# Feed-forward units two by two over two PSUM banks, and the rotation done on raw tiles ahead of the head norm

## The reference, cut to what matters

```python
def rmsnorm(x, w):
    y = xf * lax.rsqrt(jnp.mean(xf * xf, axis=-1, keepdims=True) + EPS) * w
def rope(x, pos):
    x1, x2 = xf[..., : hd // 2], xf[..., hd // 2:]
    return concatenate([x1 * cos - x2 * sin, x2 * cos + x1 * sin], axis=-1)
...
    xn = rmsnorm(x, norm_mix)
    z = xn @ w_in
    q = rope(rmsnorm(zq.reshape(B, T, SWA_HEADS, SWA_HEAD_DIM), q_norm), pos)
    k = rope(rmsnorm(zk.reshape(B, T, SWA_KV_HEADS, SWA_HEAD_DIM), k_norm), pos)
    ...
    h = rmsnorm(x, norm_ffn) @ w_up
    x = x + jnp.square(jax.nn.relu(h)) @ w_down
```

## Time and profile before

| | |
|---|---|
| time before, median of 3 runs | 950.02 us (949.9 to 950.58) |
| profiled execution, its own time | 949.91 us |
| span of that execution, first to last instruction | 948.1 us |
| busy: PE, PEld, DVE, ACT, POOL | 99%, 96%, 71%, 51%, 5% of the span |
| chain that ended last | PE 97%, of it L413 into `pz` 90% and into `pm` 6% |
| read from and written to HBM | 153.29 MB and 10.29 MB, 173 GB/s |

### The profile page before, as it was taken

The page is one execution under the profiler, slowest core; times in us unless marked ns, Lnnn a source line. Parts: engine busy times, 40 slices in busy tenths (PEclk is TensorE's granted clock), DMA queues, the critical chain, the costliest instruction groups (busy, mean ns, idle before and its releaser), DMA issues.

```text
span 948.1 us, 18976 instructions
## 1 busy us (share of the span) xinstructions
PE 943.3 (99%) x7944; PEld 914.9 (96%) x7944; DVE 669.3 (71%) x1052; ACT 483.8 (51%) x707; POOL 43.2 (5%) x61
## 2 busy tenths in 40 slices
PE   9999999999999999999999999999999999999998
PEld 8999898999999999999999998989999999999998
DVE  6798798858876755555757887889498676556463
ACT  6429663473664353535553586436537644435351
POOL 0070000000000000000001500000000000000000
PEclk9999999999999999999999999999999999999999
DMA  9655444444554585455475563534444546555542
GB/s 361 219 186 172 184 145 134 135 134 152 156 182 153 192 300 176 156 172 161 162 253 164 189 219 113 166 123 147 135 145 156 182 147 244 172 163 172 160 155 91
DMA packets 44276, 164.25 MB, mean 173 GB/s; under 512 B 4992, under 2 KB 6528, under 8 KB 43648
## 3 DMA queue, kind: packets, MB, share of 16 engines
q1 hardware_dynamic: 42912, 152.95, 49.1%
q0 software_dynamic: 1136, 9.83, 2.7%
q10 hardware_dynamic: 144, 0.26, 0.1%
HBM read 153.29 MB, written 10.29 MB: 173 GB/s over the span
## 4 chain that ended last, share of the span: by engine, by line
PE 97%; DMA 1%; ACT 0%; SPq 0%; DVE 0%; issue 0%; DVEq 0%; ACTq 0%
PE pz L413 90%; PE pm L413 6%; DMA raw<-in_w 1%; PE pm L579 1%; ACT w_hi L783 0%; DVE arena L1022 0%; PE pm L632 0%; PE pm L642 0%; SPq L356 0%; SPq L350 0%; PE pm L531 0%; SPq L360 0%; DVE arena L1054 0%; DVE xp L1058 0%; ACT rstd L801 0%
## 5 line engine op out<-in xcount | busy, mean ns | idle before, releaser
L413 PE MATMUL pz<-a_hi,w_hi 128*128 128x288 f32 x1376 | 413.2, 300 | 0.9 <-DVE a_lo L1027 0.6
L413 PE MATMUL pz<-a_lo,w_hi 128*128 128x288 f32 x1376 | 405.9, 295 | 0.0
L413 PE MATMUL pz<-a_hi,w_lo 128*128 128x288 f32 x1376 | 404.8, 294 | 0.0
L783 ACT ACTIVATE w_hi<-raw 128x1024 fp32r<-128x1024 f32 x266 | 278.0, 1052 | 208.5 <-PE pz L413 196.7
L1013 DVE TENSOR_TENSOR w_lo<-raw,w_hi 128x1024 fp32r<-128x1024 f32 x266 | 327.4, 1231 | 10.8 <-ACT w_hi L783 10.8
L413 PEld LDWEIGHTS pz<-a_hi,w_hi 128*128 128x128 f32 x1376 | 257.9, 187 | 10.5 <-issue 8.6
L413 PEld LDWEIGHTS pz<-a_hi,w_lo 128*128 128x128 f32 x1376 | 259.0, 188 | 0.0
L413 PEld LDWEIGHTS pz<-a_lo,w_hi 128*128 128x128 f32 x1376 | 258.3, 188 | 0.3
L413 PE MATMUL pz<-h_hi,w_hi 128*128 128x288 f32 x768 | 228.2, 297 | 0.0
L413 PE MATMUL pz<-h_lo,w_hi 128*128 128x288 f32 x768 | 226.5, 295 | 0.0
L413 PE MATMUL pz<-h_hi,w_lo 128*128 128x288 f32 x768 | 225.8, 294 | 0.0
(11 more groups left out here) (175 smaller groups left out, 539.9 us busy)
## 6 DMA issues: line engine op xcount, KB each, us to landing
raw<-in_w SPq DMA_DIRECT2D x267, 512.0 KB, 3.5
arena<-in_s SPq DMA_DIRECT2D x2, 2048.0 KB, 9.6
out_ss_out<-arena POOLq DMA_DIRECT2D x2, 2048.0 KB, 8.1
out_u_out<-arena POOLq DMA_DIRECT2D x2, 864.0 KB, 6.8
arena<-arena SPq DMA_DIRECT2D x8, 180.0 KB, 3.2
arena<-in_kcT SPq DMA_DIRECT2D x2, 512.0 KB, 6.9
arena<-in_vc SPq DMA_DIRECT2D x2, 512.0 KB, 7.6
out_kc_out<-in_kc_kept POOLq DMA_DIRECT2D x1, 992.0 KB, 7.0
```

The source lines that it names most:

```text
L413: return nc.tensor.matmul(out, a, b, start=start, stop=stop, **kw)
L783: act_fn(w_hi[:, r], raw[:, r], ACT.Copy).then_inc(s["w_hi"], 1)
```

## The change

**Feed-forward.** From the third unit of a layer's feed-forward part on, units j and j + 1 (j even) are computed together by `pair`: at each k-step hi*hi of both, hi*lo of both, lo*hi of both, into two banks, 48 matmuls. Only units 0 and 1 of the first turn and 12 to 15 of the last (`SINGLE` = 12) stay single. A pair waits once, for the second unit's weights and the second unit's bank. DVE does the split of unit j + 3 ahead of unit j's ReLU or addition when j is even (`early`), and after it when j is odd, as before; ACT's program is as it was. `new_state` on PE comes after the pairs (6, 7) and (12, 13), where it came after units 7 and 12.

**Rotation.** The DMAs that swap halves stand behind the load of unit 11 instead of 13 and take the raw tiles. DVE multiplies the raw tiles by weight and cosine at unit 5, the swapped ones by swapped weight and sine at unit 6, adds at unit 7 (`cos_t`), and multiplies by the spread inverse roots last, at unit 7, into `qk`. All that waited for `qk_rope` waits for `qk_norm`, which now means the finished tile. Two parameter columns per layer (the swapped weights) are new.

The diff, cut to its core:

```diff
+                    if u == 11:
+                        sp.wait_ge(s["z_read_dve"], read_dve(l, U_K))
-                    if u == 13:
-                        sp.wait_ge(s["qk_norm"], 3 * l + 3)
                         sp.sem_inc(s["sp_passed"], 1)
                         for r in range(0, P, 32):
...
+            def pair(outs, g, rhs_hi, rhs_lo, have=None):
+                hi, lo = ([w[:, (g + n) % RING].rearrange("p (k c) -> p k c", k=KT) for n in range(2)]
+                          for w in (w_hi, w_lo))
+                for k in range(KT):
+                    if have is not None:
+                        have(k)
+                    for n in range(2):
+                        mm(outs[n], hi[n][:, k], rhs_hi(k), start=k == 0, stop=False)
+                    for n in range(2):
+                        mm(outs[n], hi[n][:, k], rhs_lo(k), start=False, stop=False)
+                    for n in range(2):
+                        last = mm(outs[n], lo[n][:, k], rhs_hi(k), start=False, stop=k == KT - 1)
+                        if k == KT - 1:
+                            last.then_inc(s["unit_done"], 1)
...
+                for j in range(0, 16, 2):
                     u = U_FFN + j
+                    single = (first and j == 0) or (last and j >= SINGLE)
...
+                    for n in ((0, 1) if single else (1,)):
+                        pe.wait_ge(s["w_lo"], l * UNITS + i * 16 + (u + n + 1) + HEAD)
+                        pe.wait_ge(s["z_read_dve"], i * 16 + read_dve(l, T_FFN + j + n - 4))
+                        if single:
+                            product(outs[n:n + 1], l * UNITS + u + n, rhs_hi, rhs_lo, KT, have)
...
+                        else:
+                            pair(outs, l * UNITS + u, rhs_hi, rhs_lo, have)
+                    if first and j in (6, 12):
+                        new_state(l, 0 if j == 6 else 4)
...
+                if u in (5, 6):
+                    src, turned, table, done = ((qk, "", cos, "qk_cos"), (sin_t, "_turned", sin, "qk_sin"))[u - 5]
+                    dst = cos_t if u == 5 else sin_t
+                    if u == 5:
+                        dve.wait_ge(s["z_read_dve"], read_dve(l, U_K))
+                        dve.wait_ge(s["cos_sin_landed"], 16 * (l + 1))
+                    else:
+                        dve.wait_ge(s["qk_turned"], 64 * (l + 1))
+                    stt(dst[:, 0:4 * T].rearrange("p (j t) -> p j t", j=4), src[:, 0:4 * T].rearrange("p (j t) -> p j t", j=4),
+                        pr(l, "qw" + turned), bc(table, 4), ALU.mult, ALU.mult).then_inc(s[done], 1)
...
+                    tt(cos_t, cos_t, sin_t, ALU.add).then_inc(s["qk_turn"], 1)
...
+                    tt(qk[:, 0:3 * QR].rearrange("p (b n) -> p b n", b=3), cos_t[:, 0:3 * QR].rearrange("p (b n) -> p b n", b=3),
+                       pm[:, 0:3, 0:QR], ALU.mult).then_inc(s["qk_norm"], 1)
...
+                    g = l * UNITS + U_FFN + i * 16 + j + LEAD
+                    early = j % 2 == 0 and not (i == 0 and j == 0) and not (last and j >= SINGLE)
+                    if early and g < DEPTH * UNITS:
+                        split(g)
                     if j < 8:
...
-                    if g < DEPTH * UNITS:
+                    if not early and g < DEPTH * UNITS:
                         split(g)
```

More of the change, by code:

```diff
@@ L70 @@
 LEAD = 3
+SINGLE = 12
 UW = 1024
@@ L393, in _ @@
                 sp.sem_inc(s["sp_passed"], 1)
-                sp.wait_ge(s["qk_rope"], l + 1)
+                sp.wait_ge(s["qk_norm"], 3 * l + 3)
                 sp.sem_inc(s["sp_passed"], 1)
@@ L533, in attention @@
                 if u == 11:
-                    pe.wait_ge(s["qk_rope"], l + 1)
+                    pe.wait_ge(s["qk_norm"], 3 * l + 3)
                     pe.wait_ge(s["v_tok"], 2 * l + 2)
@@ L731, in new_state, with ffn_turn @@
                     mm(PM[h], ktok_s[rows], imask[rows, q:q + 4].rearrange("p b n -> p (b n)")).then_inc(s["snew"], 1)
-            def ffn_turn(l, i, first=False):
-                for j in range(16):
+            def ffn_turn(l, i, first, last):
+                for j in range(0, 16, 2):
                     u = U_FFN + j
-                    pe.wait_ge(s["w_lo"], l * UNITS + i * 16 + (u + 1) + HEAD)
-                    pe.wait_ge(s["z_read_dve"], i * 16 + read_dve(l, T_FFN + j - 4))
-                    out = [PZ[bank(l, T_FFN + j)][:, 0:T]]
+                    single = (first and j == 0) or (last and j >= SINGLE)
@@ L739, in ffn_turn @@
                     if j < 8:
-                        have = (lambda k: pe.wait_ge(s["a_lo"], l * 16 + (9 + k))) if first and j == 0 else None
-                        product(out, l * UNITS + u, lambda k: a_hi[:, k], lambda k: a_lo[:, k], KT, have)
-                    else:
-                        have = (lambda k: pe.wait_ge(s["f_lo"], l * 8 * FI + i * 8 + (k + 1) + HEAD)) if j == 8 else None
-                        product(out, l * UNITS + u, lambda k: h_hi[:, k], lambda k: h_lo[:, k], KT, have)
+                        rhs_hi, rhs_lo = (lambda k: a_hi[:, k]), (lambda k: a_lo[:, k])
+                    else:
+                        rhs_hi, rhs_lo = (lambda k: h_hi[:, k]), (lambda k: h_lo[:, k])
@@ L745, in ffn_turn @@
+                    have = None
                     if first and j == 0:
-                        norm_sum(2 * l + 2)
-                    if first and j in (7, 12):
-                        new_state(l, 0 if j == 7 else 4)
+                        have = lambda k: pe.wait_ge(s["a_lo"], l * 16 + (9 + k))
+                    if j == 8:
+                        have = lambda k: pe.wait_ge(s["f_lo"], l * 8 * FI + i * 8 + (k + 1) + HEAD)
+                    outs = [PZ[bank(l, T_FFN + j + n)][:, 0:T] for n in range(2)]
@@ new lines, in ffn_turn @@
+                    for n in ((0, 1) if single else (1,)):
[3 more added lines that the diff above has]
+                            product(outs[n:n + 1], l * UNITS + u + n, rhs_hi, rhs_lo, KT, have)
+                            if first and j == 0 and n == 0:
+                                norm_sum(2 * l + 2)
+                                have = None
+                        else:
+                            pair(outs, l * UNITS + u, rhs_hi, rhs_lo, have)
@@ L763, in _ @@
                 for i in range(FI):
-                    ffn_turn(l, i, first=i == 0)
+                    ffn_turn(l, i, i == 0, i == FI - 1)
         @block.scalar
@@ L1065, in attention @@
[L1065 to L1071, removed]
@@ L1081, in attention @@
+                    for a, b in ((3 * QR, 4 * T), (4 * T, 5 * T)):
+                        tt(qk[:, a:b], cos_t[:, a:b], PM[3][:, a - 3 * QR:b - 3 * QR], ALU.mult).then_inc(s["qk_norm"], 1)
                 for k in {11: (0, 1), 12: (2, 3), 13: (4, 5)}.get(u, ()):
```

25 lines of the change are left out of this document (12 added, 13 removed).

## The result

The changed kernel takes **953.47 us** (median of 7 runs, 952.74 to 954.64), beside 950.04 for the kernel before in the same rounds (7 runs, 949.74 to 950.58): a ratio of 1.0035, interval [1.0025, 1.0045]. It is slower by 3.4 us, over the upper end of the range, where no difference was forecast. The profiled execution took 952.74 us, 2.83 more than that of before, and its span is 2.8 longer than in the earlier trace rows. It was the quickest of the seven, so what it shows is the low end.

The account below looks back on a forecast made before the run. The prediction took PE's matmul spacing, 133.3 ns a step, to bound the kernel. It summed 949.91 + 0 (pairs on PE) + 0.8 (waits on DVE and ACT) + 0 (rotation) = 950.7 us, range 949.0 to 953.0.

Parts of the forecast that it names:

- the placement rival: New parameter columns move tiles behind `x` 32 bytes; 1 ns a matmul would give 957 or 944 us; chance 0.03.
- the prediction's own estimate of a sweep: On PE, a pooling matmul step of 242 ns taken as two sweeps over 288 columns gives 121 ns each.
- weights that come late after unit 7: Feed-forward: eight pairs following pair (6, 7) each lose 0.3 us to late weights, giving the range's upper end, 953.
- Part three: Rotation: DVE's work is regrouped, swapped halves land in time; 0 us, between -0.3 and +1.
- The 1 us of cover at the transposes: Rotation: `qk_norm` is done later, leaving 1 us of 2.7 before PE's transposes of the values need it.
- the rotation makes PE wait: Swapped halves landing 8 us late hold up unit 10's split; 1 to 3 us a layer, about 954; chance 0.02.
- Part two: Pairs' effect on DVE and ACT: waits at unit 2 and pair (14, 15) of each first turn, +0.8 us.
- the chain of five handovers: From a pair's end through ACT and DVE to weights for the pair after next; 0.7 us of 6.4 to spare.
- the 17 us rival: Second unit's weights late in every pair: 0.3 us in each of 58 if chain 1 us longer, 968; chance 0.10.
- Part one: Pairs on PE: same matmuls and loads in another order, spacing stays 133.3 ns, 12.80 us for 96; 0 us.
- The single step at the change of bank: Between units in the old trace, 361.47 to 361.61, within rounding 133.3 ns; taken to show alternating banks saves nothing.

Follow-up runs that it names:

- e1: Kernel before with an unused tile of 8 floats, so the operand tiles and all behind start 32 bytes later; 954.02 us, ratio 1.0042.
- e6: Kernel before with the feed-forward pairs alone, no rotation, and tiles 32 bytes later; 953.18 us, ratio 1.0033.
- e14: Kernel before with the rotation alone and tiles 64 bytes later; 945.69 us, ratio 0.9957.
- e4: Kernel before with the rotation alone, padded so that alignment within 128 bytes is as before; 951.99 us, ratio 1.0024.
- e3: Kernel before with the feed-forward pairs alone, no rotation, no tile moved; 949.69 us, ratio 0.9998.
- e10: Kernel before with the feed-forward pairs alone and tiles 64 bytes later; 945.70 us, ratio 0.9954.
- e12: Kernel before with pairs alone, tiles 64 bytes later, and units 2 and 3 of each first turn single too; 945.13 us, ratio 0.9948.
- e2: The whole changed kernel with a pad of 24 floats that restores the alignment of the kernel before; 950.87 us, ratio 1.0009 to that kernel.
- e5: Kernel before with an unused tile of 16 floats, so all tiles behind `xp` start 64 bytes later; 943.78 us, ratio 0.9936.
- e15: Kernel before with the rotation alone, tiles 64 bytes later, swap DMAs behind the load of unit 10 instead of 11; 943.85 us, ratio 0.9938.
- e13: Kernel before with the weight tiles alone moved 64 bytes, later tiles unmoved within 128 bytes; 943.80 us, ratio 0.9936.
- e16: Kernel before with the four operand tiles alone moved 64 bytes, later tiles back in place; 944.00 us, ratio 0.9937.

## Why the prediction was wrong

**The step that failed first** is the placement rival. Its mechanism and even its size were on paper ("1 ns on each of the 6432 matmuls would be 6.4 us either way: 957 or 944"), and the runs went almost to both ends: 954.0 at 32 bytes, 943.8 at 64. But it got a chance of 0.03, and the forecast took 0, on no other ground than that no row shows another placement. Absence of a row is no reason for 0: one move of tiles was certain from the diff, and a spacing 12.3 ns over the prediction's own estimate of a sweep (121 ns, if a step of the pooling matmuls is two sweeps, which no run tested) was a sign that something else sits in it. Measured: +4.2 us on the kernel before (e1). Pairs give 0.8 of it back at that place (e6 beside e1). That the time passed the range by only 0.5 us is luck: the range's upper end was reckoned from weights that come late after unit 7, and none did.

**Part three** was wrong by a size that mattered. It took 5.3 us for the swap from the second layer, behind unit 13, and moved it to unit 11 of both layers. There it takes 7.2 us in the second and 8.8 in the first layer, up to 10.3 in e14, with weight loads just ahead of it and the DMA engines 91 and 97% busy. The 1 us of cover at the transposes was reckoned rightly, and it is gone: 0.8 us of wait in the profiled run, 1.8 to 2.2 in e4 and e14. DVE's wait for the halves, said to be gone, is 2.54 us. The rival "the rotation makes PE wait" had about the price (1 to 3 us a layer) but another wait, the split of unit 10, and asked for a landing 8 us late; 3.5 were enough to hold up the transposes. The first layer was never worked out by itself.

**Part two** held. 0.35 us a layer at unit 2 was measured as 0.3 in PEld's list; of 0.05 at pair (14, 15) nothing shows; no other pair waits. DVE's second split of a pair ended 5.3 us after the pair (5.4 reckoned) at 342.77 in the second turn:

```profile
341.54 1.23 DVE L1042 TENSOR_TENSOR w_lo<-raw,w_hi 128x1024 fp32r<-128x1024 f32 x1 [0.53 <-ACT w_hi L812]
```

So the chain of five handovers was sized well enough to rule out the 17 us rival.

**Part one** came true in its number, 12.80 us for 96 matmuls, and that is luck: at this place single units would take 134.4 ns, and the pairs happen to give back 1.0. At the old place, which the prediction took, the pairs save 0.3 ns a matmul (133.0, e3), and at 64 they lose 0.4 to 0.8 (132.6 in e10 and 133.0 in e12, for 132.2). So the 0 for the pair itself was wrong by small amounts of either sign. The single step at the change of bank could not show that. A pair changes the banks and also the order of weights and operands; which of the two counts, no run separates.

**The sum** by medians: 950.0 + 4.2 (placement, e1) - 0.8 (pairs at that place, with their waits, e6 less e1) + 0.3 (rotation, the change less e6, across two sets of runs) = 953.7, for 953.47 measured. This sum closes by construction, since each term is the difference of one run to the next. The rotation's 0.3 is a net: e6 waits 0.4 us for `qk_rope` in the second layer, which the change does not. At the old place the parts measured by themselves are -0.2 (e3) and +2.1 (e4), and together +1.0 (e2): they don't add up closely, and the scatter of the runs with the rotation leaves it open whether they should.

The version that beats both kernels is the kernel before with 16 unused floats (e5), 943.78 us, 0.64% faster. None of the runs with pairs or rotation is faster than that; e15 is level with it.

## What to carry to other kernels

A change that adds a column to a table moves every tile behind it: before its parts are judged, hold the tiles still with a pad, or run the old kernel with the pad alone. Where a stream of matmuls is the bound, as here at 133.3 ns a step, trying the operands at several distances from the weights is cheap, and here it was worth more than the whole rewrite. A transfer that is moved is priced at its new place in each layer, by the transfers just ahead of it and the DMA share there, not by its old duration.

## What the hardware showed that was not expected

- The step of matmuls of 288 columns, each with its own weight load, depends on where moving operand and weights stand to each other: 133.3, 134.4, 132.2 and 132.2 ns in one and the same stretch at 0, 32, 64 and 96 bytes, at a granted clock of 1.00 in all. The period of 128 bytes rests on runs at 0 and at 128, and holds for the mean step alone: the six steps of before and of e4 differ one by one (134.5 and 133.0 for the fifth).
- In these runs the distance between the two tiles counts: moving the weights alone by 64 bytes changes the step by 1.1 ns (133.3 to 132.2) and the time by 6.0 us (e13), moving the operands alone by 64 does the same (e16), and in the steps beside idle engines the difference is about the same (133.3 ns before, 132.3 in e5). What causes it, no run shows.
- At 32 bytes the drift is uneven: the output product of the second layer ran at 133.3 ns in the profile of e1 and at 134.4 in that of the changed kernel, at the same place; in e6 it was the first layer's that ran at 134.4. What decides between them stays open.
- Pairs over two banks in turn change the step by 1.0 ns down (32 bytes, e6) to 0.4 and 0.8 up (64 bytes, e10 and e12) in the second turn of the first layer; whether the banks or the order of weights and operands do it, no run shows.
- Four SBUF-to-SBUF transfers of 180 KB each, 0.72 MB in all, took 5.2 to 10.3 us from first issue to use where DVE waited for them in the profiled runs: 5.2 to 6.4 with the last weight load some 6 us ahead (5.3 to 5.4 in the kernel before, 6.4 in e10), 7.2 to 10.3 with weight loads just ahead of them.
